# One more seven-product unit in most feed-forward pairs, with some of its weight sums moved to GpSimd

## What is computed

```python
def swiglu(h, w_gate, w_up, w_down):
    return (jax.nn.silu(h @ w_gate) * (h @ w_up)) @ w_down

h = rmsnorm(x, ffn1_norm)                                    # x: (1, 256, 2048)
x = x + 0.5 * swiglu(h, ffn1_w_gate, ffn1_w_up, ffn1_w_down) # gate, up: (2048, 5504); down: (5504, 2048)
...                                                          # mixer, cross attention
x = x + 0.5 * swiglu(rmsnorm(x, ffn2_norm), ffn2_w_gate, ffn2_w_up, ffn2_w_down)
```

## Time and profile before

| | us |
|---|---|
| median of 3 runs (lowest to highest) | 1874.12 (1873.51 to 1874.81) |
| the profiled execution, its own time | 1873.65 |
| its span in the trace | 1871.5 |
| PE busy | 1865.0 |
| DVE busy | 1632.0 |
| ACT busy | 1117.8 |
| POOL busy | 96.1 |

### The profile page before, as it was taken

The page is one execution under the profiler, slowest core; times in us unless marked ns, Lnnn a source line. Parts: engine busy times, 40 slices in busy tenths (PEclk is TensorE's granted clock), DMA queues, the critical chain, the costliest instruction groups (busy, mean ns, idle before and its releaser), DMA issues.

```text
span 1871.5 us, 23391 instructions
## 1 busy us (share of the span) xinstructions
PE 1865.0 (100%) x8772; PEld 1565.2 (84%) x8772; DVE 1632.0 (87%) x2098; ACT 1117.8 (60%) x1500; POOL 96.1 (5%) x98
## 2 busy tenths in 40 slices
PE   9999999999999999999999999999999999999999
PEld 8888888888889888988888888888888888888987
DVE  6999998899999978787676774799999999999997
ACT  7675665556666547556476655666665555656654
POOL 0000000000000002312260000000000000000000
PEclk9999999999999999999999999999999999999999
DMA  9665655665566674456443654456565666565664
GB/s 341 224 219 175 212 203 195 212 213 197 175 199 220 209 242 148 145 173 221 137 156 112 208 193 140 158 169 213 170 210 196 208 203 214 197 200 187 202 197 158
DMA packets 176033, 362.57 MB, mean 194 GB/s; under 512 B 8880, under 2 KB 20144, under 8 KB 175280
## 3 DMA queue, kind: packets, MB, share of 16 engines
q1 hardware_dynamic: 175488, 360.89, 58.0%
q10 hardware_dynamic: 432, 0.19, 0.0%
HBM read 358.95 MB, written 2.10 MB: 193 GB/s over the span
## 4 chain that ended last, share of the span: by engine, by line
PE 54%; DVE 0%; issue 0%; DVEq 0%
PE acc L2142 9%; PE acc L2140 9%; PE acc L2141 9%; PE acc L2129 6%; PE acc L2131 6%; PE acc L2130 6%; PE small L2142 1%; PE small L2140 1%; PE small L2141 1%; PE tr L2088 1%; PE small L2356 1%; PE tr L2142 1%; PE tr L2140 1%; PE tr L2141 1%; PE tr L2156 1%; PE small L2567 0%
## 5 line engine op out<-in xcount | busy, mean ns | idle before, releaser
L1388 DVE TENSOR_TENSOR w_lo<-w_raw,w_hi 128x1024 fp32r<-128x1024 f32 (+3 forms) x776 | 793.8, 1061 | 41.2 <-ACT w_hi L768 17.5
L779 ACT ACTIVATE w_hi<-w_raw 128x1024 fp32r<-128x1024 f32 (+2 forms) x456 | 414.1, 943 | 97.5 <-PE acc L2142 74.3
L2140 PE MATMUL acc<-w_hi,hT_hi 128*128 128x512 f32 (+1 forms) x912 | 352.0, 386 | 0.0
L2142 PE MATMUL acc<-w_lo,hT_hi 128*128 128x512 f32 (+1 forms) x912 | 350.1, 384 | 0.0
L2141 PE MATMUL acc<-w_hi,hT_lo 128*128 128x512 f32 (+1 forms) x912 | 349.9, 384 | 0.0
L885 ACT ACTIVATE w_hi<-w_raw 128x1024 fp32r<-128x1024 f32 (+1 forms) x216 | 222.7, 1043 | 99.8 <-DVE w_raw L1398 66.0
L878 ACT ACTIVATE w_hi<-w_raw 128x512 fp32r<-128x512 f32 (+1 forms) x216 | 176.6, 834 | 139.2 <-PE acc L2142 135.7
L1320 DVE TENSOR_TENSOR w_lo<-w_raw,w_hi 128x1024 fp32r<-128x1024 f32 (+1 forms) x166 | 197.2, 1230 | 24.4 <-ACT w_hi L779 22.9
L2140 PE MATMUL acc<-w_hi,actT_hi 128*128 128x512 f32 x508 | 198.4, 391 | 0.4 <-DVE w_lo L1388 0.4
L2140 PEld LDWEIGHTS acc<-w_hi,hT_hi 128*128 128x128 f32 x912 | 171.2, 188 | 32.5 <-DVE w_lo L1388 1.2
L2142 PEld LDWEIGHTS acc<-w_lo,hT_hi 128*128 128x128 f32 x912 | 171.2, 188 | 32.2
(11 more groups left out here) (354 smaller groups left out, 2816.8 us busy)
## 6 DMA issues: line engine op xcount, KB each, us to landing
w_raw<-in_ffn_w_gate SPq DMA_DIRECT2D x98, 512.0 KB, 3.8
w_raw<-in_ffn_w_down SPq DMA_DIRECT2D x56, 768.0 KB, 4.3
w_raw<-in_ffn_w_down SPq DMA_DIRECT2D x36, 1024.0 KB, 5.2
w_raw<-in_ffn_w_up SPq DMA_DIRECT2D x34, 1024.0 KB, 5.1
w_raw<-in_ffn_w_up SPq DMA_DIRECT2D x62, 512.0 KB, 4.9
w_raw<-in_w_in SPq DMA_DIRECT2D x29, 1024.0 KB, 5.1
w_raw<-in_ffn_w_gate SPq DMA_DIRECT2D x22, 768.0 KB, 4.4
w_raw<-in_ffn_w_up SPq DMA_DIRECT2D x22, 768.0 KB, 5.7
```

The source lines that it names most:

```text
L779: nc.scalar.activation(piece(w_hi, c % SPLIT, k0, k1, width), piece(raw, c % RAW, k0, k1, width), ACT.Copy).then_inc(hi_done, 1)
L1388: return v.tensor_tensor(piece(w_lo, c % RAW, k0, k1, width), piece(raw, c % RAW, k0, k1, width), piece(w_hi, c % SPLIT, k0, k1, width).bi ...
L2140: mm(dst, lhs_hi, wh, start=first, stop=False, skip_group_check=goes_on)
L2142: return mm(dst, lhs_hi, wl, start=False, stop=last, skip_group_check=goes_on)
```

## The change

Every up pair now uses `UP4`. The down pairs of half 0 have six units in place of five, with first-side slots of 2 tiles and later slots of 4. The token sums of the sixth unit are made too (`A_SUMS` 5 becomes 6). GpSimd takes over two kinds of weight sums, in `weight_sums`:

- `next_sums(m)`, for every up pair: the `first_sums` of the next pair's first unit. It waits, besides its data, for the split of the first later slot and for `first_part`, after which DVE does `take_parts` and `take_first`.
- `side_sum(m)`, for every up pair but the first of a feed-forward step: one of the two tiles of the second unit's `first_sums`. It waits for DVE's tile and for PE's end of the pair before, when DVE does `take_second`. ACT's `hi_made` and DVE's `other_raw` wait for it.

DVE's `take_first` of an up pair moves from the end to right behind `take_parts`. In the first pair of a step DVE's `first_sums` of the second unit moves behind the gate multiply (L1499). The norm of the memory on GpSimd moves behind the third pair.

```diff
-    H_SUMS, A_SUMS = 4, (5, 4)
+    H_SUMS, A_SUMS = 4, (6, 4)
...
-        UP3 = ("upupup", [0, 2, 4], [(6, 4), (10, 3), (13, 3)], [(6, 4), (10, 3), (13, 3)])
-        FOUR = [(0, 2), (0, 4), (1, 1), (1, 3)]
         UP4 = ("upupupup", [0, 2, 4, 6], [(8, 2), (10, 2), (12, 2), (14, 2)], [(8, 4), (12, 4)])
-        DOWN = [("upupupupup", [0, 2, 4, 6, 8], 2 * [(10, 3), (13, 3), (16, 3), (19, 3), (22, 2)]),
+        DOWN = [("upupupupupup", [0, 2, 4, 6, 8, 10], [(12, 2), (14, 2), (16, 2), (18, 2), (20, 2), (22, 2)] + [(12, 4), (16, 4), (20, 4)]),
...
+            def next_sums(m):
+                d, e = DUOS[m], DUOS[m + 1]
+                c, n = e.raws[0], unit_number(m + 1, 0)
+                b, made = weight_tiles(c, e.width), weight_tiles(c + 1, e.width)
+                pool.wait_ge(loaded[c % RAW], landed(c))
+                pool.wait_ge(slot_used, 2 * (c + 1 - RAW + 1))
+                pool.wait_ge(lo_done, 2 * d.seconds[0] + 2)
+                pool.wait_ge(ev("combined"), 2 * n)
+                pool.wait_ge(ev("first_part"), m + 1)
+                nc.gpsimd.tensor_tensor(made[:, 0:2, :], b[:, 1:4:2, :], b[:, 0:2, :], ALU.subtract).then_inc(ev("combined"), 1)
+            def side_sum(m):
...
+                pool.wait_ge(ev("combined"), 2 * n + 1)
+                pool.wait_ge(slot_used, 2 * DUOS[m - 1].end)
+                nc.gpsimd.tensor_tensor(made[:, 1, :], b[:, 3, :], b[:, 1, :], ALU.subtract).then_inc(ev("side_sum"), 1)
...
-                    first_sums(d.raws[1], w)
+                    if m > m0:
+                        first_sums(d.raws[1], w, tiles=1 if has_side(m) else 2)
                     if m == m0:
...
                         dve.sem_inc(ev("nat_done"), 1)
+                        first_sums(d.raws[1], w)
...
+                        if n == 1 and has_side(m):
+                            dve.wait_ge(ev("side_sum"), side_number(m) + 1)
                         other_raw(d.raws[n], u0 + n, w)
...
-                            if m < LAST[f]:
+                            if m < LAST[f] and not d.up:
                                 first_sums(DUOS[m + 1].raws[0], DUOS[m + 1].width)
...
                             take_parts(m)
+                            if d.up:
+                                take_first(m)
```

More of the change, by code:

```diff
@@ L272, in layer @@
         hS_sum = at("hS_sum", A0 + 56, [P, H_SUMS, 4, P])
-        aS_hi = at("aS_hi", A0 + 64, [P, 5, 3, P], F32R)
-        aS_los = [at(f"aS_lo{n}", A0 + 71.5 + 1.5 * n, [P, 3, P], F32R) for n in range(4)]
-        aS_sums = [at(f"aS_sum{n}", A0 + 71.5 + 1.5 * n, [P, 3, P]) for n in range(4)]
+        aS_hi = at("aS_hi", A0 + 64, [P, 6, 3, P], F32R)
+        aS_los = [at(f"aS_lo{n}", A0 + 73.0 + 1.5 * n, [P, 3, P], F32R) for n in range(5)]
+        aS_sums = [at(f"aS_sum{n}", A0 + 73.0 + 1.5 * n, [P, 3, P]) for n in range(5)]
         aS_los.append(nc.alloc_sbuf_tensor_at("aS_lo_late", [P, 3, P], F32R, offset=late))
@@ L361, in number_ffn @@
                 for b in range(1 - h, -(-tiles // 4)):
-                    DUOS.append(Duo(f, True, h, b, min(4, tiles - 4 * b) * P, *(UP4 if (h, b) in FOUR else UP3)))
+                    DUOS.append(Duo(f, True, h, b, min(4, tiles - 4 * b) * P, *UP4))
                 for j in range(DB // 2):
@@ L478, in up_number, with has_side, side_number @@
             return sum(d.up for d in DUOS[:m])
+        def has_side(m):
+            return DUOS[m].up and m not in FIRST.values()
+        def side_number(m):
+            return sum(has_side(k) for k in range(m))
         def new_sums(m):
@@ L708, in differences, with weight_tiles, weight_sums @@
                 nc.gpsimd.tensor_tensor(w[:, :, 0, :], mid, b[:, :, 0, :], ALU.subtract).then_inc(ev("differences"), 1)
+            def weight_tiles(c, width):
+                return raw[:, c % RAW, :].rearrange("p (k n) -> p k n", k=4)[:, :, 0:width]
+            def next_sums(m):
[9 more added lines that the diff above has]
+            def side_sum(m):
+                d = DUOS[m]
+                c, n = d.raws[1], unit_number(m, 1)
+                b, made = weight_tiles(c, d.width), weight_tiles(c + 1, d.width)
+                pool.wait_ge(loaded[c % RAW], landed(c))
+                pool.wait_ge(slot_used, 2 * (c + 1 - RAW + 1))
+                pool.wait_ge(ev("combined"), 2 * n + 1)
+                pool.wait_ge(slot_used, 2 * DUOS[m - 1].end)
+                nc.gpsimd.tensor_tensor(made[:, 1, :], b[:, 3, :], b[:, 1, :], ALU.subtract).then_inc(ev("side_sum"), 1)
+            def weight_sums(f):
+                for m in range(FIRST[f], LAST[f] + 1):
+                    if has_side(m):
+                        side_sum(m)
+                    if DUOS[m].up:
+                        next_sums(m)
+                    if m == FIRST[1] + 2:
+                        norm("mem")
             done(nc.gpsimd.memset(half[:], -0.5))
@@ L712, in _ @@
             norm("x1")
-            norm("mem")
+            weight_sums(1)
             norm("x2")
@@ L754, in _ @@
             norm("x4")
+            weight_sums(2)
         @block.scalar
@@ L878, in hi_raw, with hi_made @@
                     nc.scalar.activation(piece(w_hi, c % SPLIT, k0, k1, width), piece(raw, c % RAW, k0, k1, width), ACT.Copy).then_inc(hi_done, 1)
-            def hi_made(c, n, width, made="combined"):
+            def hi_made(c, n, width, made="combined", side=0):
                 for i, (k0, k1) in enumerate(MADE_PARTS):
                     act.wait_ge(ev(made), 2 * n + i + 1)
+                    if side and i == 0:
+                        act.wait_ge(ev("side_sum"), side)
                     act.wait_ge(slot_used, freed(c, i))
@@ L918, in duos @@
                             hi_raw(d.raws[n], w)
-                            hi_made(d.raws[n] + 1, u0 + n, w)
+                            hi_made(d.raws[n] + 1, u0 + n, w, side=side_number(m) + 1 if n == 1 and has_side(m) else 0)
                         if kind == "p":
@@ L1376, in weight_tiles, with first_sums @@
                 return raw[:, c % RAW, :].rearrange("p (k n) -> p k n", k=4)[:, :, 0:width]
-            def first_sums(c, width, made_sem="combined"):
+            def first_sums(c, width, made_sem="combined", tiles=2):
                 b, made = weight_tiles(c, width), weight_tiles(c + 1, width)
@@ L1537, in duos @@
                             take_parts(m)
+                            if d.up:
+                                take_first(m)
                         if m == LAST[1] and n in (1, 2):
                             turned_lo(hT_hi, hT_lo, 4 * (n - 1), groups["x_in"] + n - 1, 0, splits["x_in"] + n - 1, 0, gain=col["mix_norm"])
-                    take_first(m)
+                    if not d.up:
+                        take_first(m)
                     if m < LAST[f]:
```

4 lines of the change are left out of this document (2 added, 2 removed).

## The result

The changed kernel takes 1884.85 us (median of 4 runs, 1884.35 to 1884.95) against 1873.82 us before (4 runs, 1873.3 to 1874.81): a ratio of 1.0059, 95% interval 1.0047 to 1.0072. It is 11 us slower. That lies in the predicted range (1867.5 to 1886), but not at the predicted 1874.5, and in the band of rival 2 (1878 to 1886).

The account below looks back on a forecast made before the run. PE's matmul stream was taken as the bound; 10.57 us saved against 10.7 of waits and 0.4 of release gaps gave net +0.5 on 1873.65, 1874.1, and with 0.47 to the median 1874.5 us; range 1867.5 to 1886.

Parts of the forecast that it names:

- rival 2: Behind take_second, a late side_sum holds the port against DVE's split; 1880 us at a 0.6 us miss, chance 0.20.
- Saving on PE: Feed-forward pairs: each new unit saves three matmuls, 10.57 us in all, all on the path.
- First pairs: First pair of each step, now four units: PE waits for DVE's splits, 2.64 us in step 1, 2.53 in step 2.
- Middle up pairs just fit: Four-unit up pairs in a row: no stall, 0.28 us of DVE's reserve to spare in each, lasting 41.8 us.
- `take_first` adds nothing to DVE: In up pairs, moving take_first before two splits with 2.4 us or more of reserve adds no DVE time.
- The reserve as a price cut: Side_sum collision in 18 pairs: the 0.28 us reserve (split end to waiting matmul) was deducted from each pair's price.
- First down pair: First down pair of each step, behind a four-unit pair: PE waits 2.2 us for DVE, 4.4 in all.
- 384-wide pair: Third plain slot of each step's 384-wide up pair: reserve falls to -0.67 us, counted as 0.6 twice, 1.2.
- next_sums is free under 3.2 us: GpSimd's next_sums, some 2.1 us, fits under DVE's take_parts and take_first, 3.2 us, so costs nothing.
- Rival 3: GpSimd's side_sum is starved by DVE's splits and DVE idles at other_raw: 14 us more, 1888 us, chance 0.10.
- Rival 1: Waits at the pairs' edges are smaller: 1868.7 us if only first pairs stall, 1863.6 with none; chance 0.20.
- waits of PE below 5 us in the list: PE's list of waits: below 5 us would mean Rival 1 holds; 9 to 11 us for DVE's split was expected.

Follow-up runs that it names:

- e2: Changed kernel with side_sum waiting only for VectorE's last split of the pair's first unit, so requested earlier: 1881.64 us.
- e3b: Changed kernel with the first addition of take_first in up pairs no longer waiting for the last addition of take_parts: 1882.08 us.
- v1: Changed kernel with side_sum earlier, take_first's wait dropped, five-unit half-0 down pairs, three-unit first and 384-wide pairs, second mem load later: 1869.66 us.
- e7: Changed kernel with three units again in only the 384-wide up pair of each step: 1883.89 us.
- e6: Changed kernel with the second 1 MB load of mem behind the second pair's first late slot, its squares and norm one pair later: 1883.41 us.
- e8: Changed kernel with side_sum waiting for VectorE's take_second instead of PE's end of the pair, so requested later: 1897.38 us.
- e9: Changed kernel with no weight sums on GpSimd, VectorE making them where it did before: 1904.04 us.

## Why the prediction was right in some steps and wrong in others

- *Saving on PE, 10.57 us:* right where nobody waits. The second down pair went from 61.88 us with five units to 61.20 with six: 0.68 = 3 x 0.227.
- *First pairs, 2.53 and 2.64 us of waits:* right in size. That of step 1, 43.65 us before, should have become 43.65 - 0.68 + 2.54 = 45.5, and is 45.53. In the kernels that leave it alone it is 46.0 to 46.4, as its first matmul comes up to 0.7 us earlier or its end up to 0.6 later; why is open, so the agreement to a tenth is luck. In step 2 the pair went from 42.44 to 44.55 us, 2.1 more instead of 1.85, so 2.8 us of waits instead of 2.5.
- *Middle up pairs just fit, with 0.28 us to spare in each:* wrong, and the main error. Two steps failed. The first is a term: `side_sum` was taken at 1.04 us and starting 0.1 us after DVE's sum; it takes 1.30 (the mixer's operation had one full operand and a broadcast one, this one has two full ones; no run changes only that) and starts 0.23 us after the end of DVE's sum, 0.32 us into `take_second`. The argument that both wait for the same event failed with it: DVE is late in these pairs, so DVE's own sum is what releases GpSimd. The cover was measured with the wrong row and from the wrong start. It is 0.42 us short, which costs 0.28 us (e2). The second is "`take_first` adds nothing to DVE": it was put directly behind an operation for which it waits, 0.18 us (e3b). v1 has both out and runs at 41.81, so the ledger itself was sound.
- *The reserve as a price cut:* wrong in kind. I deducted 0.28 us from the price in each pair. A reserve is there once; in a row of four-unit pairs nothing refills it, and then each pair pays the whole price: 0.46 us, 42.3 for 41.8. Rival 2's own formula makes the same mistake: a miss of 0.42 us less 0.28 of reserve would have cost 2.5 us in 18 pairs. With the right price, 0.46 in each of 11 pairs, rival 2 and the self-wait give 5.1 us, and 5.7 were measured.
- *First down pair, 2.2 us each:* nearly right; it lost 2.7. PE waits there also for `take_second` (0.6 us at L1480), which stands behind a sum of 1.13 us on two tiles. I followed only the splits.
- *384-wide pair, 0.6 each:* 0.9. The down pair behind it had no term at all, because I judged the pairs by the third plain slot and took DVE to enter the next pair as before; it lost 0.7. Three units in the 384-wide pair give that back in step 1; in step 2 a late `next_sums` takes it away again (e7).
- *next_sums is free under 3.2 us:* right where its weights are there: 127.83 to 130.25 in a middle pair, with `take_parts` and `take_first` from 127.53 to 130.85. Wrong in the first pair of step 1, where its DMA comes late (e6), 2.1 us. The same happens behind a 384-wide pair of three units (e7, v1). I had named the queue's order nowhere: two late slots instead of three move the next unit's load up to the loads of `mem`.
- *Rival 2:* the time fell into its band, but the collision of `side_sum`, 3.1 us, is less than a third of the 11 us. The rest is the self-wait (2.0), the late `next_sums` (2.1) and smaller misses at the edges. That they add up to rival 2's band is luck.
- *Rival 3:* for `side_sum` refuted by e8. *Rival 1:* no pair had smaller waits. The sign that I gave for it, waits of PE below 5 us in the list, did appear (4.7 for L1434) and was a false sign, as the list shows only a part of the lost time.
- *Small slips:* the longest wait of PE in the kernel before is not 0.6 us but 1.0, once in the mixer, which the change doesn't touch. The sum comes to 1874.6 and not 1874.5, and the 384-wide pair's -0.67 was counted as 0.6.
- *The factor of two:* the Trainium skill (GPSIMD Engine Reference, section 4.1 Engine selection) advises against two-input elementwise work on GpSimd, which it calls about two times slower. The trace agrees on the factor, 1.30 us against 0.60. Against the advice, the work is better placed on GpSimd here, where DVE has no time left and the sums are not waited for: e9, without GpSimd, is 19.2 us slower.

## What to carry to other kernels

Time the cover and what it covers from rows of the very operand kinds involved, and from the start that semaphores allow, not from the event that releases both. Reserve is a stock: spread over many like pairs, a loss of a few tenths is paid in full in each, so alternate heavy and light pairs or bring the heavy one below the other engine's pace. When an edit shortens a sequence of slots, look at what the DMA queue has between them, and at how long before its use the next load is requested.
